# Branch weights in chunks of 512 columns, pool products among the cache values, attention products added to them in place

## The reference

```python
z = xn @ w_in                       # u | q | k | v | gates, 1024 x 7168
pool_o = pool_branch(u, ...)        # 512 wide
att_o  = combine_groups(...)        # 512 wide, needs the cache values
g = sigmoid(gates)                  # two gates of 1024
h = g[..., 0, :] * (pool_o @ w_bp) + g[..., 1, :] * (att_o @ w_ba)
x = x + h @ w_o
```

## Time and profile before

| | |
|---|---|
| median of 3 runs | 2075.82 us (2075.54 to 2080.75) |
| the profiled execution | 2075.19 us, of which its span is 2073.4 us |
| granted TensorE clock, mean over the span | 0.972 of full speed |
| PE busy | 1972.2 us, 95% of the span |
| DMA, mean | 267 GB/s |
| chain that ended last | PE 89%, DMA 4%, DVE 3%, ACT 2%, issue 1% |
| the stretch, layer 0 | 286.43 us (G0 begins) to 406.28 us (`w_out` begins) |
| the stretch, layer 1 | 924.51 us to 1041.79 us |

### The profile page before, as it was taken

How to read it: one execution, slowest core, us unless ns; L and a number is a source line. 1 busy time by engine, 2 the same in 40 slices (tenths; PEclk the granted TensorE clock), 3 DMA queues, 4 the chain that set the end, 5 groups by cost and what they waited for, 6 DMA issues and landing times.

```text
span 2073.4 us, 45436 instructions
## 1 busy us (share of the span) xinstructions
PE 1972.2 (95%) x20817; PEld 1350.1 (65%) x20818; DVE 617.8 (30%) x1033; ACT 492.4 (24%) x753; POOL 146.2 (7%) x221
## 2 busy tenths in 40 slices
PE   6998988999998998988998999999999999999997
PEld 5988866989998997876895353534435353444434
DVE  4445532554435454641452011010101001010111
ACT  3434432344433443531331000000000000000000
POOL 0113100102210111300000000000000000000000
PEclk9999999999999999999999999999999999999998
DMA  7443579645544443478834999999999999999995
GB/s 237 153 143 113 188 263 311 224 140 163 163 163 159 145 146 136 150 238 300 268 128 127 374 388 357 396 371 383 366 383 377 367 394 362 387 374 378 365 384 198
DMA packets 211588, 552.68 MB, mean 267 GB/s; under 512 B 11220, under 2 KB 107516, under 8 KB 194866
## 3 DMA queue, kind: packets, MB, share of 16 engines
q1 hardware_dynamic: 207184, 541.67, 72.2%
q0 software_dynamic: 3072, 8.00, 1.1%
q10 hardware_dynamic: 1138, 0.06, 0.0%
HBM read 542.28 MB, written 7.76 MB: 265 GB/s over the span
## 4 chain that ended last, share of the span: by engine, by line
PE 89%; DMA 4%; DVE 3%; ACT 2%; issue 1%; POOL 0%; SPq 0%; DVEq 0%; ACTq 0%; POOLq 0%
PE psum L849 83%; PE psum L857 7%; DMA low_part<-in_w_in 3%; ACT w_split L1395 1%; DVE w_split L1650 1%; DMA out_kv_prompt<-high_part 0%; DMA high_part<-in_const_a 0%; DVE high_part L1657 0%; DVE high_part L1643 0%; DVE low_part L1742 0%; DVE high_part L1747 0%; ACT low_part L1429 0%; DVE low_part L2070 0%; POOL high_part L2183 0%; DVE low_part L1643 0%
## 5 line engine op out<-in xcount | busy, mean ns | idle before, releaser
L849 PE MATMUL psum<-low_part 128*32 128x512 f32 (+3 forms) x6926 | 684.8, 528 | 6.7 <-DVE high_part L1643 5.0
L849 PE MATMUL psum<-xn_split,w_split 128*128 128x288 f32 x3744 | 528.2, 302 | 38.7 <-DVE w_split L1650 19.2
L849 PEld LDWEIGHTS psum<-xn_split,w_split 128*128 128x128 f32 x3744 | 514.2, 192 | 63.2 <-DVE w_split L1650 32.4
L849 PEld LDWEIGHTS psum<-low_part 128*32 128x32 f32 (+2 forms) x6926 | 239.1, 114 | 385.0 <-issue 373.4
L849 PE MATMUL psum<-low_part,high_part 128*32 128x256 f32 (+3 forms) x6636 | 355.1, 362 | 8.0 <-POOL high_part L2186 4.9
L1650 DVE TENSOR_TENSOR w_split<-low_part,w_split 128x2048 fp32r<-128x2048 f32 x105 | 241.0, 2295 | 397.6 <-ACT w_split L1395 397.6
L849 PEld LDWEIGHTS psum<-low_part,high_part 128*32 128x32 f32 (+1 forms) x6636 | 220.8, 113 | 134.5 <-issue 23.8
L1395 ACT ACTIVATE w_split<-low_part 128x2048 fp32r<-128x2048 f32 x105 | 201.1, 1915 | 384.4 <-PE psum L849 252.8
L857 PE MATMUL psum<-high_part,low_part 128*128 128x128 f32 (+3 forms) x1001 | 141.3, 287 | 18.2 <-DMA high_part<-in_const_a 9.3
L857 PEld LDWEIGHTS psum<-high_part,low_part 128*128 128x128 f32 (+3 forms) x1001 | 113.3, 145 | 59.7 <-issue 42.4
L1375 ACT ACTIVATE high_part<-psum 128x384 f32<-128x384 f32 (+2 forms) x72 | 35.9, 498 | 468.5 <-PE psum L857 437.1
(11 more groups left out here) (134 smaller groups left out, 999.3 us busy)
## 6 DMA issues: line engine op xcount, KB each, us to landing
low_part<-in_we_down SPq DMA_DIRECT2D x112, 1024.0 KB, 7.6
low_part<-in_cache_kv_g SPq DMA_DIRECT2D x72, 1024.0 KB, 5.5
low_part<-in_we_gate SPq DMA_DIRECT2D x64, 1024.0 KB, 8.0
low_part<-in_we_up SPq DMA_DIRECT2D x64, 1024.0 KB, 7.2
low_part<-in_w_in SPq DMA_DIRECT2D x56, 1024.0 KB, 5.1
low_part<-in_we_gate SPq DMA_DIRECT2D x64, 768.0 KB, 6.0
low_part<-in_we_up SPq DMA_DIRECT2D x64, 768.0 KB, 6.7
low_part<-in_w_dense SPq DMA_DIRECT2D x33, 1024.0 KB, 5.2
```

The source lines that it names most:

```text
L849: signal(e.matmul(out, lhsT, rhs, start=start, stop=stop, skip_group_check=mixed), inc)
```

## The change

Branch weights are now chunks of one weight each, 512 rows x 512 columns. Two of them (P0, P1) are pool weights and stand as steps among gates and values: P0 behind G3's value steps, P1 behind G7. `V_BEHIND` gets an entry for each of the ten steps: two value steps behind each of G0 to G4 and P0, three behind G5 and G6, none behind G7 and P1. The two attention chunks (A0, A1) follow P1. Still 48 matmuls per chunk and the same sums; a row of a branch chunk in memory is 2 KB in place of 1 KB. The pool tiles take banks from `SIX` now.

VectorE writes the pool product of a tile straight into `merged` in the P steps, and the attention product into `prod`; GpSimd adds it to `merged` in place.

```diff
+W_STEPS = [("G", 0), ("G", 1), ("G", 2), ("G", 3), ("P", 0), ("G", 4), ("G", 5), ("G", 6), ("G", 7), ("P", 1)]
+V_BEHIND = (2, 2, 2, 2, 2, 2, 3, 3, 0, 0)
...
-EX0_GATE = 4
+EX0_STEP = 5
...
+        if kind == "P":
+            js += [(("pb", 4 * n + x), SIX) for x in range(4)]
+            continue
...
+    js += [(("ab", c), None) for c in range(KT)]
...
+                    else:
+                        send(L, c, [(view(slot(c), 4, 512), columns(io["w_branch_pool"][L], 512 * n, 512))])
...
+                for i in range(2):
+                    send(L, c, [(view(slot(c), 4, 512), columns(io["w_branch_attn"][L], 512 * i, 512))])
...
+                def branch(b, w, i):
+                    w = chunk(L, w).rearrange("p a (k n) -> p a k n", k=4)
+                    e.wait_ge(bl_ready.sem, bl_ready.at(L, b + 1))
+                    for x in range(4):
+                        project(S, (("pb", "ab")[b], 4 * i + x), lambda a, k: w[:, a, k, 128 * x:128 * (x + 1)],
+                                [branch_split[b][:, a] for a in range(2)], 4)
+                    done.append(split_used)
...
+                for i in range(2):
                     split_high(L, W_BRANCH + i + 1)
-                    for c in ((2 * i - 2, 2 * i - 1) if i else ()):
+                    for c in range(4 * i, 4 * i + 4):
                         merge_high(e, L, c)
...
+                    split_low(L, W_MERGE + s + 1)
+                    if s == 0:
                         new_probs(1)
-                    elif n == 3:
+                    elif s == 3:
                         branch_low(0, poolT)
...
+                    if kind == "P":
+                        for c in range(4 * n, 4 * n + 4):
+                            gated_branch(0, c, merged[:, c, :])
+                split_low(L, W_BRANCH + 1)
+                for c in range(KT):
+                    if c >= 4:
+                        e.wait_ge(merged_ready.sem, merged_ready.at(L, c - 3))
+                    gated_branch(1, c, prod[c % 4])
+                    if c >= 2:
+                        merge_low(c - 2)
+                    if c == 5:
+                        split_low(L, W_OUT)
...
-                    e.tensor_tensor(merged[:, c, :], prod[(2 * c) % 4], prod[(2 * c + 1) % 4], ALU.add)\
+                    e.tensor_tensor(merged[:, c, :], merged[:, c, :], prod[c % 4], ALU.add)\
```

More of the change, by code:

```diff
@@ L126, in chunk_kinds @@
 def chunk_kinds():
-    steps = ["W" if kind == "G" else "C" for kind, _ in V_STEPS]
-    return ["W"] * N_IN + ["C"] * (N_CACHE // 2) + steps + ["W"] * (KT + N_DENSE)
+    steps = ["C" if kind == "V" else "W" for kind, _ in V_STEPS]
+    return ["W"] * N_IN + ["C"] * (N_CACHE // 2) + steps + ["W"] * (2 + KT // 2 + N_DENSE)
 class Tally:
@@ L367, in hidden_place @@
     return 3 + (f - 12) % 4, (f - 12) // 4
-DMAS = [1] * (N_IN + N_CACHE + KT) + [2] * (KT // 2) + [1] * (KT // 2 + N_DENSE)
+DMAS = [1] * N_LAYER
 assert len(DMAS) == N_LAYER
@@ L1140, in attention @@
                         continue
-                    gates(n)
-                    if n == 0:
+                    s = W_STEPS.index((kind, n))
+                    if kind == "P":
+                        branch(0, W_MERGE + s, n)
+                        continue
+                    gates(s, n)
+                    if s == 0:
                         turn_s_probs(1)
-                    elif n == EX0_GATE:
+                    elif s == EX0_STEP:
                         gather_heads(0)
[L1147 to L1155, removed]
+                for i in range(2):
+                    branch(1, W_BRANCH + i, i)
                 for c in range(KT):
@@ L1498, in attention @@
                 sample_exp(e, L, 1)
-                for n in range(KT):
-                    split_high(L, W_MERGE + n + 1)
-                    for x in range(2):
+                for s, (kind, n) in enumerate(W_STEPS):
+                    split_high(L, W_MERGE + s + 1)
+                    for x in range(2 if kind == "G" else 0):
                         job = (f"g{n % 2}", n // 2 * 2 + x)
@@ L1876, in merge_low, with gated_branch @@
                         .then_inc(ml_ready.sem, 1)
-                for n in range(KT):
-                    if n == EX0_GATE:
+                def gated_branch(b, c, out):
+                    job = (("pb", "ab")[b], c)
+                    S.wait_read(e, (f"g{b}", c))
+                    S.wait_full(e, job)
+                    S.freed(e.tensor_tensor(out, gate[2 * c + b], S.ps(job)[:, 0:T], ALU.mult), job)
+                for s, (kind, n) in enumerate(W_STEPS):
+                    if s == EX0_STEP:
```

67 lines of the change are left out of this document (23 added, 44 removed).

## The result

The changed kernel is slower: a median of 2082.81 us over 20 runs (2077.18 to 2092.05) against 2078.59 over 20 of the kernel before, ratio 1.0024 with a 95% interval of 1.0013 to 1.0034: a small loss, but clear of the noise. The forecast was 2075, no change.

A forecast was written before the change was run, and what follows sets the result against it. With matmuls filling 95% of the span, time could come only from TensorE's waits or lower clock. Layers -3.6 and -1.1, falls +2.0 each, sum to -0.7 us: 2075 from 2075.82, own range 2071 to 2079, with rivals 2064 to 2083.

The forecast's parts named there:

- where the waits stand: Sign: waits before G2 to G5 under 2 us, P0 waiting for `branch_low`, 3 to 4 us before G6 and G7.
- a fall behind G6's wait is hidden: At G6: a clock fall there costs nothing, as G7 waits for its weights anyway.
- the 3.7: Before G7: TensorE free at 370.6, weights ready at 374.3, a wait of 3.7 us.
- G6's wait of 3.1: Before G6: TensorE free at 358.1, weights ready at 361.2, a wait of 3.1 us.
- V14 lands at 354.0: Value chunk just ahead of G6's weights: lands at 354.0, and G6's weights at 356.9.
- P0's wait: Before P0: TensorE free at 325.4, start at 327.8 behind split and `branch_low(0)`, a wait of 2.4 us.
- one uncovered fall per layer at 2.0: Gate stretch: one clock fall per layer that nothing hides, costing 2.0 us, the mean of those seen.
- two dear falls: Rival, chance 0.17: clock falls at P0 and G7, each at 2.5 us, 6.0 more in all, 2081 us.
- the tail: Behind P1, to `w_out`: added waits at A0, a `w_out` split and `w_out`, 2.0 us against 0.2 before.
- The pieces of 2 KB: Branch chunk transfers: by the rows no gain; by the skill page P0's wait shrinks by at most 2.4 per layer.
- Last transfers sooner: Rival, chance 0.27: V16 and V17 landed when G7 is issued, G7 lands 5.4 later, wait 0.7, no fall: 2065 us.
- Transfers set the pace: Rival, chance 0.09: chunks take 3.3 us each whatever the order, 0.2 per layer over the sum: 2075.4 us.

The follow-up runs named there:

- order undone: Changed kernel with the old step order (eight gates, then both pool steps), 512-column chunks and in-place products kept: 2083.06 us, ratio 1.0034 to before.
- moved trios: Changed kernel with shortened tail, value trios behind G0 and P0, pool low part before P0's split, weights asked one place earlier: 2058.27 us, ratio 0.9916 to before.
- short tail: Changed kernel with attention products and `w_out` taking banks from 6 on and the first `w_out` chunk split sooner: 2080.61 us, ratio 1.0025 to before.
- P0 alone early: Changed kernel with only P0's weights asked for one place earlier and the pool low part before their split: 2078.64 us, ratio 1.0015 to before.
- weights asked early: Changed kernel with each weight chunk of the stretch asked for one place earlier, ahead of the last value chunk before it: 2069.95 us, ratio 0.9963 to before.
- branch low: Changed kernel with the low part of the pool branch computed before the split of P0's weights: 2081.78 us, ratio 1.0033 to before.
- trios moved: Changed kernel with the two trios of value steps moved from behind G5 and G6 to behind G0 and P0: 2094.70 us, ratio 1.0092 to before.

## Why the prediction was wrong

**Right: where the waits stand.** G2 to G5 wait under 1.2 us; P0 waits for `branch_low(0)` behind its split. VectorE in layer 0, first profile, P0 starting at 331.55:

```profile
327.89 2.29 DVE L1656 TENSOR_TENSOR w_split<-low_part,w_split 128x2048 fp32r<-128x2048 f32 x1 [7.72 <-ACT w_split L1403]
330.10 1.35 DVE L1876 TENSOR_TENSOR pool_branch_split<-low_part,pool_branch_split 128x1152 fp32r<-128x1152 f32 x1
```

**Right: a fall behind G6's wait is hidden.** G7's weights are asked for once G6 has begun (366.94 in the first profile, layer 0) and land 7.5 us later, however long G6's step takes. The chain of work that ended last, followed from G6's weights to G7's first matmuls (start, length, what), doesn't hold G6's step at all:

```profile
352.61 10.03 DMA low_part<-in_w_in
362.66 1.92 ACT w_split L1403
364.60 2.30 DVE w_split L1656
367.58 7.49 DMA low_part<-in_w_in
375.09 1.92 ACT w_split L1403
377.04 2.30 DVE w_split L1656
379.38 4.28 PE psum L852 x32
```

G7 begins 12.1 to 13.2 us after G6 in the ten layers (forecast 13.1). G6's step took 8.71 to 9.08 in all six layers of the three profiles, 2.3 over 6.66 in the mean, and G7's wait, with the 0.32 of the gathering, shrank to 0.8 to 1.8. The mean of that, 1.4, and the 2.3 make the 3.7 that was forecast as wait alone.

**The step that failed: G6's wait of 3.1, from "V14 lands at 354.0".** That puts V14's landing at 5.4 us. In all ten layers it took 7.0 to 7.7 (the line of 352.20 above), although the chunk before it had landed. G6's weights came 2.9 to 3.2 us behind V14, as counted, so the wait was 5.0 to 5.7, mean 5.3: 2.2 more per layer, and nothing hides it. The earlier trace rows held a value chunk with 7.0; the prediction used it for V16 and not for V14.

**Two smaller terms in the same stretch.** P0's wait, forecast at 2.4, was 3.1 in the mean of six layers, since its weights, behind V7, took 6.8 to 7.9 us in three of them where 5.5 was put. "I count one uncovered fall per layer at 2.0" came out at 1.2: P0's step fell in three of six layers, by 2.2 to 2.5, and G7's in none. The rival *two dear falls* (2081) had P0's fall; its second, at G7, did not come, so that its time lies near the measured one is luck.

**A term mis-sized: the tail.** Forecast 2.0 against 0.2, so 1.8; measured 2.35 (order undone). Between first matmuls A0 comes 0.9 later than without a wait (forecast 0.8), `w_out` 0.9 (forecast 0.6), and `w_out` itself is 0.53 longer (forecast 0.6). What was left out is at `w_out`: the 0.63 of its wait was counted, the drain of the matmuls before it, about 0.3, was not. VectorE in layer 0 shows the split of the first `w_out` chunk in front of the last two products:

```profile
405.63 2.49 DVE L1656 TENSOR_TENSOR w_split<-low_part,w_split 128x2048 fp32r<-128x2048 f32 x1 [0.33 <-ACT w_split L1403]
408.05 0.44 DVE L1888 TENSOR_TENSOR low_part<-low_part,psum 128x288 f32<-128x288 f32 x1
408.41 0.45 DVE L1881 TENSOR_TENSOR merged_low<-high_part,merged_high 128x288 fp32r<-128x288 f32 x1
408.78 0.44 DVE L1888 TENSOR_TENSOR low_part<-low_part,psum 128x288 f32<-128x288 f32 x1
```

**The sum.** Per layer: 2.2 at G6, 0.7 at P0, 0.8 less for falls, 0.2 less before G2 and G3, 0.5 in the tail: 2.4 more than forecast. Measured are 2.6 more, 146.54 us against 144.0 (half of 288.63 less 0.7). In the first profile the counted fall did not come, and G6's wait was 2.4 and 1.9 longer than forecast: that its 0.72 less met the forecast of 0.7 less was luck.

**The pieces of 2 KB** show no gain: P0's chunk landed in 5.3 to 7.9 us, `w_in` chunks with pieces of 1 KB in 5.1, and P0's wait did not shrink. The Trainium skill, page Perfetto Trace Analysis, section DMA Optimizations, would have had them faster; no run here changes the size of the pieces alone.

**The other rivals.** *Last transfers sooner*: G7's weights took 7.1 to 8.3 us in the ten layers, not 5.4, with V17 still 4.1 to 5.1 us from landing when they were issued. *Transfers set the pace* is not what held the changed kernel back, since asking earlier gains, and with moved trios the waits that were left mostly went too.

**Open.** The two ratios mean 5.0 and 8.1 us; 3.4 of them are found between G0 and the end of `w_out`. Outside, the three profiles of before average 1787.1 us (span less those parts) and those of after 1791.7; but the variants, with the same code there, run from 1783.5 to 1795.6, so whether anything of that belongs to the change isn't settled. No run shows why V14 takes 7 us or more with the chunk before it landed, nor why P0's chunk comes 2.6 to 3.0 us behind V7 at one time and 4.4 to 5.0 at another. And the runs that shorten one term alone (short tail, P0 alone early) move the time by less than their intervals, so the terms rest on the timelines more than on the times.

## What to carry to other kernels

One profile shows one execution: where it agrees with the forecast in the total, compare the terms too, since two errors can cancel. Price a wait by the landing of the very transfer that it hangs on, and take the longer of two landings in the rows unless something speaks for the shorter. A slow step cost nothing here where the next step waited for a transfer that didn't depend on it. When products are merged in turn instead of in pairs, count the drains at the seam, and which engine's split stands in front of the last of them. In this kernel it paid to ask for a weight chunk, which must be split first, ahead of data that needs no preparation: the order of the transfers need not be the order of use.

## What the hardware showed that was not expected

Waits of 1.86 and 1.95 us before P0 (weights asked early) were followed by steps of 5.59 and 7.46 us, or of 7.95, where 4.83 and 6.66 are usual, while 3.10 us in another run (branch low first) were not: the length of the last wait alone doesn't tell whether the clock falls. And an engine that only drains can hold up the one that computes: with the trios moved, one split on ScalarE that waited 10.84 us for its transfer held back two sigmoids of 0.69 us together, then TensorE for 3.34 us, and the value steps behind ran at half speed.
